# Latent attention's rotated scores: one fp32 product as two fp32r products of split tiles

## The reference, cut to what matters

```python
q = (_rms(cq, q_a_norm) @ w_uq).reshape(B, T, MLA_HEADS, MLA_QK)          # MLA_QK = 128 + 64
kv = (_rms(ckv, kv_a_norm) @ w_ukv).reshape(B, T, MLA_HEADS, MLA_NOPE + MLA_V)
k_nope, v = kv[..., :MLA_NOPE], kv[..., MLA_NOPE:]
k = jnp.concatenate([k_nope, jnp.broadcast_to(k_rope[:, :, None, :], (B, T, MLA_HEADS, MLA_ROPE))], axis=-1)
q = _rms(q, q_norm)
k = _rms(k, k_norm)
q = jnp.concatenate([q[..., :MLA_NOPE], _axial_rope(q[..., MLA_NOPE:], row, col)], axis=-1)
k = jnp.concatenate([k[..., :MLA_NOPE], _axial_rope(k[..., MLA_NOPE:], row, col)], axis=-1)
s = jnp.einsum('bqhd,bkhd->bhqk', q, k).astype(jnp.float32) * (MLA_QK ** -0.5)
p = jax.nn.softmax(s, axis=-1).astype(v.dtype)
o = jnp.einsum('bhqk,bkhd->bqhd', p, v)
```

## Time and profile before

| | us |
|---|---|
| median of 3 executions | 2357.22 (2355.9 to 2360.34) |
| the profiled execution, as timed | 2356.58 |
| its span, first to last instruction | 2354.9 |
| PE busy in the span | 2284.3 (97%) |
| latent stage from its first key-rank sum to the merge, 1541 to 1813 | 272 |

### The profile page before, as it was taken

One profiled execution on the slowest core, in us unless ns is written; L12 is line 12 of the kernel. 1 busy time (PEld: TensorE's weight loads), 2 busy tenths in 40 slices (PEclk: granted clock), 3 DMA queues, 4 the chain that ended last, 5 costly groups with the idle time before them and its releaser, 6 DMA issues.

```text
span 2354.9 us, 29410 instructions
## 1 busy us (share of the span) xinstructions
PE 2284.3 (97%) x11742; PEld 1857.3 (79%) x11742; DVE 1299.2 (55%) x2022; ACT 961.6 (41%) x1691; POOL 364.0 (15%) x343
## 2 busy tenths in 40 slices
PE   8999999999999989999899999999999999999999
PEld 6777878778788867899788898776666888888887
DVE  5664664377665456666676676335555534542432
ACT  4354444443222236544455444354544423431331
POOL 1002050131011121223332223111111001000000
PEclk9999999999999989999999999999999999999999
DMA  5211332245554222111110101111001433223232
GB/s 199 90 54 63 109 114 83 99 138 184 178 197 152 62 91 78 57 43 50 32 41 32 46 30 57 46 46 37 26 21 56 134 103 125 90 92 96 99 99 81
DMA packets 64854, 201.91 MB, mean 86 GB/s; under 512 B 7216, under 2 KB 14144, under 8 KB 64336
## 3 DMA queue, kind: packets, MB, share of 16 engines
q1 hardware_dynamic: 64656, 199.99, 25.8%
q10 hardware_dynamic: 64, 0.05, 0.0%
HBM read 193.41 MB, written 6.60 MB: 85 GB/s over the span
## 4 chain that ended last, share of the span: by engine, by line
PE 88%; DVE 7%; ACT 2%; issue 1%; POOL 1%; DMA 0%; ACTq 0%; SPq 0%; DVEq 0%
PE ps L136 84%; PE ps L139 4%; DVE sb L175 2%; DVE sb L167 2%; DVE r L167 1%; ACT r L148 1%; ACT sb L148 1%; DVE r L175 1%; POOL sb L167 1%; POOL sb L172 0%; DVE sb L172 0%; DMA sb<-decays 0%; ACT L146 0%; DMA sb<-in_xT 0%; DVE sb L161 0%
## 5 line engine op out<-in xcount | busy, mean ns | idle before, releaser
L136 PE MATMUL ps<-r 128*128 128x512 f32 (+2 forms) x7176 | 1590.2, 380 | 34.1 <-DVE r L167 19.6
L136 PEld LDWEIGHTS ps<-r 128*128 128x128 f32 (+1 forms) x7176 | 1280.9, 189 | 299.3 <-DVE r L167 29.1
L136 PE MATMUL ps<-sb 128*128 128x128 f32 (+6 forms) x3564 | 664.2, 332 | 30.9 <-ACT sb L148 13.9
L167 DVE TENSOR_TENSOR r<-sb,r 128x1024 fp32r<-128x1024 f32 (+3 forms) x397 | 422.0, 1073 | 436.5 <-ACT r L148 436.3
L148 ACT ACTIVATE r<-sb 128x1024 fp32r<-128x1024 f32 (+3 forms) x445 | 382.7, 879 | 644.2 <-PE ps L136 504.7
L136 PEld LDWEIGHTS ps<-sb 128*128 128x128 f32 (+2 forms) x3564 | 484.0, 191 | 169.5 <-issue 100.2
L167 POOL TENSOR_TENSOR sb<-sb 128x512 f32<-128x512 f32 (+3 forms) x227 | 277.2, 1226 | 1551.2 <-ACT sb L148 969.2
L148 ACT ACTIVATE sb<-ps 128x512 f32<-128x512 f32 (+4 forms) x491 | 207.0, 447 | 364.1 <-PE ps L136 211.7
L175 DVE SCALAR_TENSOR_TENSOR sb<-sb 128x512 f32<-128x512 f32 (+5 forms) x240 | 238.1, 1004 | 25.2 <-ACT sb L148 23.6
L167 DVE TENSOR_TENSOR sb<-ps,sb 128x512 f32<-128x512 f32 (+2 forms) x238 | 142.4, 607 | 141.0 <-PE ps L136 127.2
L148 ACT ACTIVATE sb<-sb 128x512 f32<-128x512 f32 (+6 forms) x339 | 176.9, 537 | 88.9 <-POOL sb L167 35.1
(11 more groups left out here) (25 smaller groups left out, 213.3 us busy)
## 6 DMA issues: line engine op xcount, KB each, us to landing
sb<-in_w_mlp SPq DMA_DIRECT2D x60, 512.0 KB, 3.5
sb<-in_w_mod SPq DMA_DIRECT2D x48, 512.0 KB, 4.4
sb<-in_w_qkv SPq DMA_DIRECT2D x24, 512.0 KB, 3.7
sb<-in_w_g SPq DMA_DIRECT2D x20, 512.0 KB, 4.4
sb<-in_w_u SPq DMA_DIRECT2D x20, 512.0 KB, 4.0
sb<-in_w_out SPq DMA_DIRECT2D x16, 512.0 KB, 3.6
sb<-in_w_down SPq DMA_DIRECT2D x16, 512.0 KB, 3.6
sb<-in_w_gate SPq DMA_DIRECT2D x16, 512.0 KB, 3.7
```

Of the source, the lines that this page charges most:

```text
L136: return QUIET if self.e is None else self.e.matmul(o, l, r, start=start, stop=stop)
L167: return QUIET if self.e is None else self.e.tensor_tensor(o, a, b, op)
```

## The change

Rotated queries and keys are split into high and low fp32r parts, and the empty half of the 128 rows is used for the split. For a head the query tile QS holds the high part in the head's own 64 partitions and the low part in the other 64. The rotated key is no longer masked: krT holds it in both halves, so the two key tiles KRH (high) and KRL (low) hold it twice. One product QS by KRL and one QS by KRH then give all four partial products, where one fp32 product stood.

```diff
-                    m = e.matmul(P(b * 512 + n0, n), S(qr + new * 128, 128), S(kh + NA + n0, n), False, True)
+                    e.matmul(P(b * 512 + n0, n), X2(qs, new * 128, 128), X2(krl, n0, n), False, False)
+                    m = e.matmul(P(b * 512 + n0, n), X2(qs, new * 128, 128), X2(krh, n0, n), False, True)
```

ACT and DVE make the parts; a first unit now waits for `qs_up` and `ks_lo`:

```diff
+            e.act(X2(QS[h % 2], 0, NT, p, 64), S(QR, NT, p=p, n=64), ACT.Copy).then_inc(*up("qs_hi", h))
+            yield
+            e.wait_ge(*at("qs_lo", h))
+            e.act(X2(QS[h % 2], 0, NT, 64 - p, 64), S(QR, NT, p=p, n=64), ACT.Copy).then_inc(*up("qs_up", h))
+            e.tt(q, q, X2(QS[h % 2], 0, NT, p, 64).bitcast(F32), SU).then_inc(*up("qs_lo", h))
+            e.act(X2(KRH[h % 2], 0, NA), S(KRL[h % 2], NA), ACT.Copy).then_inc(*up("ks_hi", h))
-            e.stt(S(kh + NA, NA), S(krT, NA), sm("half", h % 2), S(RL, NA), MU, MU).then_inc(*up("k_n", h, 1))
+            e.tt(S(KRL[h % 2], NA), S(krT, NA), S(RL, NA), MU).then_inc(*up("k_n", h, 1))
+            e.tt(X2(KRL[h % 2], 0, NA), S(KRL[h % 2], NA), X2(KRH[h % 2], 0, NA).bitcast(F32), SU).then_inc(*up("ks_lo", h))
-                fence(e, [("lq_rot", h - h % 2), ("q_ev", h), ("k_n", h, 1)] + free[b] + free[b + 1])
+                fence(e, [("qs_up", h), ("q_ev", h), ("ks_lo", h)] + free[b] + free[b + 1])
```

Here `X2` addresses a tile of type fp32r (written `x` in the order below). QR is one tile instead of two; three of the new tiles lie in slots 3 and 4, so the merge's fourth and fifth chunks are loaded later:

```diff
-        chunks[first_merge + 3]["after"] = chunks[first_merge + 4]["after"] = [("w_used", CI["w_kr", 0][0])]
+        chunks[first_merge + 3]["after"] = chunks[first_merge + 4]["after"] = [("s_s", 7, 3)]
```

More of the change, by code:

```diff
@@ L56 @@
           **{tag: "end" for tag in ("p1", "p2", "p3")}, **{tag: "rot" for tag in ("qk", "rk", "lq", "lk")},
-          **{tag: "split" for tag in ("o", "y", "y1", "y2", "m", "hx", "ml", "f", "f2", "act")},
+          **{tag: "split" for tag in ("o", "qs", "ks", "y", "y1", "y2", "m", "hx", "ml", "f", "f2", "act")},
           **{tag: "soft" for tag in ("x", "s")}}
@@ L2376, in program @@
         TURNS2 = {
-            "PE": ("kkkkkkkkkkkkkkkkkkzkkzkkzzffzffzqquutfftfzfzquqntutvqvfftvtvvvftvfvtvvvvzvzqvuvvuvqvfftqzfztftqvuutn"
-                "vfftvfvvvtqfqvvqzzvqvtvvvftvtvtvvkftffvtvquvvvtqvuvvvtntvvvfntfvfvzfzvqvvqnuuvtqvffttffqvvtvvqfqutuv"
-                "vvttvtvvvvuuvvvvvnnutvvznn"),
-            "DVE": ("wnwwwwkkkwnwnKkkKkwkkffqwtvtfnnvftvttvvvtvvwvtnvfvvtvvvvqfwtttvvfKnvfvntvvvtwntvfnqfvvvtvtvvtvvvtvtt"
-                "vvffvvtvtvnnvtvvwnnvtnvvvfnfvqnntttvvfvvfvtvvtfvtvtwtvvnqvvtvvkvnwnnvwnnn"),
-            "ACT": ("wwnkwkkkkkwkwkkwkkkkkkwkknkkzwkzffffzquuqfwfffzqtutqutffqtvtfvvtwfvtvvvtzquvvquvfwfkqtnzffqtuutfftvv"
-                "fwvqfqtnqvztvqvttvvftftvtffvqvutvqtvuvvttwfnvfffvtznvqquvuvqftftfftqnvvqztuvuttwtvvwwtvutuvvvnvnfqvu"),
-            "POOL": ("nnfffnfqqffqnfffqfqnffqnffqnnfffqqn"),
+            "PE": ("kkkkkkkkkkkkkkkkkkkkqkkqzzffqquffffzztftufqtzvzvtvvvtvqfttvfvqffvvzzvvvtuqvtuvtnvvtvvvqfftvnkvuffvzu"
+                "qzntvvvtvtnqvvtqfvuvfqfufvzvzvttfuqfvtvffvtvuzzvtvqvfqvvftvqvtvffutvvuzvzfqttvqvnztvvtvvvvfqvvffvvuv"
+                "unvttnttfvvvuuvvvvtvnvquvn"),
+            "DVE": ("wwwwkkkkknkwwkKkKqqwqfffwtvtnfftvvvfvtvvtvttnqvvwvqfvfvtfvtnvvvtnnvwtvvnnvntvqffvKfnvnttnvtnvknvwtvq"
+                "vvqvfffnttvqtvwfvvftnfvvvvtvqtvqtwvvvtffvftvvtvnntqtvvvvvvvnvffnnfnttqvntvftvvvvvvnwwvtnw"),
+            "ACT": ("wwkwkkkkkkwkkwwkkkkkkkkkkkwqqzqfqfqqufqfnffwfztffqtuqftzvtvvtqfvftnwtfqfqvzqvftvquutvvwttvqnvqffvutf"
+                "fnqufkqzvvttnwvqttvqfqufvqqffuvfnzftqvuwqqtffvfvtufztvfqqfvvqtqvtwtffuvfqtufzvqtvqtvqqtvtvfqvnffvuvu"
+                "fznwntvttvtuuvvqvuwwvtfv"),
+            "POOL": ("nnqfffqfffqnnffqnqfnffnqfqffnfnqqff"),
         }
@@ L2435, in program, with X2 @@
         QH = [c + i * 512 for i in range(2)]
-        QR = [c + 1024 + i * 512 for i in range(2)]
-        KH = [c + 2048 + i * 1536 for i in range(2)]
+        QR = c + 1024
+        KH = [c + 2048 + i * 768 for i in range(2)]
+        KRH, KRL = [SLOT[3], c + 3584], [SLOT[3] + 768, c + 4352]
+        QS = [SLOT[3] + 1536, c + 1536]
+        exact = {}
+        for o, n in [(o, NA) for o in KRH + KRL] + [(o, NT) for o in QS]:
+            with ExitStack() as st:
+                st.enter_context(nc.sbuf_tensor(f"under{o}", [128, o], F32))
+                exact[o] = st.enter_context(nc.sbuf_tensor(f"x{o}", [128, n], F32R))[:, 0:1], n
+        def X2(o, at_, n, p=0, rows=128):
+            t, width = exact[o]
+            return bass.AP(t.tensor, p * width + at_, [[width, rows], [1, n]])
         VH = [c + 5120 + i * 768 for i in range(2)]
@@ L2669, in query_act @@
                 yield
+            p = 64 * (h % 2)
+            e.wait_ge(*at("lq_rot", h - h % 2))
+            if h >= 2:
+                e.wait_ge(*at("s_s", h - 2, 3))
+            e.act(X2(QS[h % 2], 0, NT, p, 64), S(QR, NT, p=p, n=64), ACT.Copy).then_inc(*up("qs_hi", h))
+            yield
+            e.wait_ge(*at("qs_lo", h))
+            e.act(X2(QS[h % 2], 0, NT, 64 - p, 64), S(QR, NT, p=p, n=64), ACT.Copy).then_inc(*up("qs_up", h))
+            yield
             e.wait_ge(*at("l_sum", "q", h))
@@ L2680, in query_dve @@
             if h % 2 == 0:
-                o = QR[h // 2 % 2]
+                o = QR
                 raw = P(BK["qr", h] * 512, NT)
@@ L2693, in query_dve @@
                 yield
+            p = 64 * (h % 2)
+            q = S(QR, NT, p=p, n=64)
+            e.wait_ge(*at("qs_hi", h))
+            e.tt(q, q, X2(QS[h % 2], 0, NT, p, 64).bitcast(F32), SU).then_inc(*up("qs_lo", h))
+            yield
         def query_pool(e, h, before):
@@ L2739, in key_act @@
                 yield
+            e.wait_ge(*at("k_n", h, 1))
+            e.act(X2(KRH[h % 2], 0, NA), S(KRL[h % 2], NA), ACT.Copy).then_inc(*up("ks_hi", h))
+            yield
         def key_dve(e, h):
@@ L2785, in score_pe @@
         def score_pe(e, h):
-            qh, qr, kh = QH[h % 2], QR[h // 2 % 2], KH[h % 2]
+            qh, qs, kh, krh, krl = (x[h % 2] for x in (QH, QS, KH, KRH, KRL))
             for new in range(4):
@@ L2933, in program @@
         assert W + 4096 <= OS and mH + 4096 <= SBW
-        latent_end = [("y2_ev", 7), ("z_y", 3, 1), ("l_o", 7), ("k_n", 7, 1), ("pt_d", 7, 3), ("pt_a", 7, 3)]
+        latent_end = [("y2_ev", 7), ("z_y", 3, 1), ("l_o", 7), ("ks_lo", 7), ("pt_d", 7, 3), ("pt_a", 7, 3)]
         def branches_of(mt):
```

8 lines of the change are left out of this document (5 added, 3 removed).

## The result

The changed kernel took 2340.71 us, the median of 4 executions (2339.7 to 2343.55), beside 2358.67 us for the kernel before (4 executions, 2355.9 to 2360.34). The ratio is 0.9927, with an interval of 0.991 to 0.9944: faster by 0.7%. The forecast was 2341.5. The profiled execution took 2339.7 us with a span of 2338.1 (before: 2356.58 and 2354.9), both at a mean granted clock of 0.993.

The account below looks back on a forecast made before the run. PE, busy 97% of the span, was taken as the bound, the latent stage as the sum of its products. 2356.6 - 18.6 (products) + 1.7 + 1.2 + 0.5 (waits) = 2341.4, forecast 2341.5 us, range 2336.5 to 2352.

Parts of the forecast that it names:

- The sum: Whole kernel: 2356.6 - 18.6 + 1.7 + 1.2 + 0.5 = 2341.4 us, forecast as a median of 2341.5.
- The net of 0.58 a unit: PE, each unit: 1.29 us removed, 0.71 added by the fp32r products; over 32 units 18.6 us saved.
- Place 1: First rank sum of squares: gate products no longer cover ACT's squares, so PE waits 1.7 us, which does not come back.
- Place 2: Keys' chain ahead of each head's first unit: longer by copy and subtraction, but hidden, by 0.7 us at the fifth head.
- Place 3, the tail: Last head: PE waits 0.2 to 0.3 us for a bank and 0.9 before the last PV, together 1.2 us.
- Small ties: Second head's key projection, seventh head's PV and places not walked: 0.5 us of waits, from 0 to 5.
- Waits as a whole: Sign to look for: PE's waits in the stage 3 to 4 us, the longest about 1.7 at the first rank sum.
- Late loads: Merge's fourth and fifth chunks, loaded after the last unit: cost nothing; without cover they would cost 6 us.
- Table loads: Rival: ACT's loads fall before exponentials that PE's work waits for, 10.3 us more, 2352; chance 0.12 with similar waits.
- The handed-on parts: Rival: ACT and DVE run late before each head's first unit, 33 us less 18.6, time 2371; chance 0.05.
- Dear products: Rival: new fp32r products run at fp32's pace, a unit takes 3.87 us, time 2398; chance 0.01.

Follow-up runs that it names:

- e1: Changed kernel with one fp32 product in place of the two fp32r products, the keys' low part left out of it; 2359.59 us, ratio to before 1.0006.
- e5: Changed kernel without the product of QS by KRL, all splits and the order kept; 2330.18 us, ratio to before 0.9886.
- e3: Changed kernel's order with the work of the kernel before: one fp32 product on masked keys, no splits; 2357.85 us, ratio to before 1.0005.
- e9: Changed kernel with PE's first query projections and values' up-projection moved earlier, ACT's query eviction and first values' copy too; 2338.92 us, ratio to before 0.992.
- e4: Changed kernel with one more ACT copy and one more DVE step in each head's key chain; 2342.94 us, ratio to before 0.9934.
- e6: Changed kernel with the eight gate evictions as copies instead of Silu, so no table loads in the stage; 2339.69 us, ratio to before 0.9924.

## Why the prediction was right

**The sum.** The forecast change of the stage was -18.6 + 1.7 + 1.2 + 0.5 = -15.2 us. It was -17.14, and the merge gave 0.26 back. The median came out at 2340.71, 0.8 under the forecast. That is closer than executions of one kernel repeat (2339.7 to 2343.55 for this one), so the 0.8 is in part luck, and the stage, 1.9 under its forecast, is the fairer measure. Read from starts, as place 3 below explains, the 1.9 are 0.7 for the tail, 0.9 for small waits of the kernel before that went with its order and that the sum had not taken off, and 0.2 for products a little cheaper than forecast, less 0.1 for the small ties. Some 0.3 stay open.

**The net of 0.58 a unit** was right: unit to unit 1.99 us for a forecast of 2.0, e1 gives 18.55 us for all of them (18.8 without the bank's wait that only the shorter units have), and e5 0.348 for a pair of products against 0.354. So the pace of a long run of the same type of product holds also for a pair that stands between fp32 products and loads new weights for each. The page "TensorE: Matmul & The Clock Gate" of the Trainium skill, section "Back-to-back issue gap", with its 131 ns for 512 columns, is not borne out: an estimate by it is 1.8 us for a unit (1.99 less two times 0.097), and the measured 1.99 decides.

**Place 1** was forecast as 1.7 us and shows as 1.48 (1539.56, for ACT), plus the 0.24 or so that a gap hides: 1.7. ACT's squares are at their old distance from the projection's end. e3 shows that the order made it and not the new steps. That it "does not come back" was right for this order, but e9 shows that 1.0 of the 1.5 can be had back by moving a few steps of PE, if ACT's move too.

**Place 2** was forecast as hidden by 0.7 at the fifth head and is hidden there by 0.9; e4's four waits show that the queue does wait there once the chain is 1.8 longer. One part was wrong: "by the same count the others have 7.5 us or more". The third head has only 0.8 of margin, and the first, fourth and sixth 1.3 to 1.6. I had counted PE's cover for every head but the chain only for one, and ACT's queue has other work ahead of the copy (there the exponentials' and the queries' steps, the third head's waited behind a gate eviction). It cost nothing, but the margin is thin in five heads and not in one.

**Place 3, the tail,** was the term that was mis-sized: forecast 1.2, measured about 0.5. Both of its waits are there, but in no bracket. A bracket counts from the end that the profile gives the last product, drain included, so a wait about as short as the drain does not show. The starts show it. PE's timeline of the changed kernel, the third unit of the last head and the end of the stage:

```profile
1791.44 0.60 PE L139 MATMUL ps<-sb 128*128 128x128 f32 x4
1792.03 1.13 PE L136 MATMUL ps<-sb 128*128 128x512 f32 x2
...
1799.90 2.32 PE L139 MATMUL ps<-sb 128*128 128x128 f32 x18
```

Four transposes between two units take 0.43 us in the kernel before (1602.01 to 1602.44), and here 0.59. The two instructions behind them start 0.53 apart instead of 0.43. That is 0.25 us for the bank, whose exponential's last record ends at 1791.97. The forecast had 0.2 to 0.3. The last values' product at 1802.25 (shown above) starts 0.30 us behind the last transpose, where 0.11 is usual, and its second instruction 0.07 late, 0.26 in all, where the forecast had 0.9. The first of the last four units starts at 1787.46 and the last copy on DVE ends at 1802.10, 14.6 us later, where PE's own work was put at 14.4 and DVE's chain at 15.3. PE's side was about right; DVE's was too long. Its timeline there:

```profile
1797.45 0.68 DVE L158 COPY sb<-ps 128x512 f32<-128x512 f32 x1
1798.05 0.15 DVE L187 RECIPROCAL sb<-sb 128x1 f32<-128x1 f32 x1
1798.23 0.62 DVE L172 TENSOR_SCALAR sb<-sb 128x768 f32<-128x768 f32 x1
1798.77 0.68 DVE L158 COPY sb<-ps 128x512 f32<-128x512 f32 x1
```

A scaling takes 0.62, not the 0.75 of the mean in the earlier trace rows (see the last section), and from start to start the copy takes 0.60 and the scaling 0.54: on DVE too, durations overlap by up to 0.1 and a chain of them is shorter than their sum.

**Small ties** were set at 0.5 and came to 0.6 by starts: 0.36 ahead of the seventh head's product with the values (four transposes from 1781.51 to 1782.23, and the late second instruction), which the prediction had named, and 0.27 at the fifth head's key sum. The kernel before had three such waits of its own, 0.31 at 1568.93, 0.43 at 1754.79 (the 0.19 of the earlier trace rows) and 0.16 at 1807.08. They went with its order. **Waits as a whole:** the signs to look for were 3 to 4 us in the stage. The view shows 1.48, the starts 2.9 (1.7, 0.25, 0.26 and 0.6, with rounding). **Late loads** were nothing, as said: no wait of PE names a DMA, and the merge is 0.3 us longer at most.

**The rivals.** Table loads: e6 takes them away and gains 0.03 us. With the 2.66 us that the page "ScalarE: Activation LUTs" of the Trainium skill, section "What ACT_TABLE_LOAD costs", gives for a switch, an estimate would be 2341.4 + 8 x 2.66 = 2362.7, some 6 us slower and not level as the prediction put it; here neither price was paid by the program. The handed-on parts: e1 less e3 gives 0.26 us for all of them together. Dear products: no.

## What to carry to other kernels

On a kernel whose bound engine is busy all the time, price an edit by start-to-start distances in unbroken runs of the same form: that term came out within 0.2 us of 18.6. For chains on the other engines, take the duration of the very instruction, not the mean of a group, and walk the chain for every repetition, not only where the cover is shortest. To find waits of 0.2 us, compare starts: the list of waits leaves them out. And when a wait at a sum is filled by moving work up, look at once at what loses that work behind it: it took three orders until the hole did not merely move, and in the first of them the clock fell as well, right behind two short waits.
